# Turning the gated feed-forward rows on VectorE instead of TensorE

## What is computed

```python
def swiglu_ffn(x, norm, w_gate, w_up, w_down):
    h = rms_norm(x, norm)
    return (jax.nn.silu(h @ w_gate) * (h @ w_up)) @ w_down      # D_FF = 2816

for l in range(DEPTH_2):                                        # 2 layers
    x = x + 0.5 * swiglu_ffn(x, ffn1_norm[l], ffn1_w_gate[l], ffn1_w_up[l], ffn1_w_down[l])
    ...                                                         # mixing
    x = x + 0.5 * swiglu_ffn(x, ffn2_norm[l], ffn2_w_gate[l], ffn2_w_up[l], ffn2_w_down[l])
```

## Time and profile before

| | |
|---|---|
| median of 3 runs | 1918.7 us (1918.16 to 1920.13) |
| span of the profiled execution, first to last instruction | 1916.1 us |
| what the median has beyond that span | 2.6 us |
| TensorE busy | 1895.2 us (99%), granted clock 0.999 |
| GpSimd busy | 1361.4 us (71%) |
| ScalarE busy | 913.7 us (48%) |
| VectorE busy | 587.1 us (31%) |
| memory read | 361.5 MB, 192 GB/s over the span |

### The profile page before, as it was taken

One profiled execution on the slowest core, in us unless ns is written; L12 is line 12 of the kernel. 1 busy time (PEld: TensorE's weight loads), 2 busy tenths in 40 slices (PEclk: granted clock), 3 DMA queues, 4 the chain that ended last, 5 costly groups with the idle time before them and its releaser, 6 DMA issues.

```text
span 1916.1 us, 25277 instructions
## 1 busy us (share of the span) xinstructions
PE 1895.2 (99%) x9754; PEld 1538.9 (80%) x9754; DVE 587.1 (31%) x1061; ACT 913.7 (48%) x1365; POOL 1361.4 (71%) x568
## 2 busy tenths in 40 slices
PE   6999999999999999999999999999999999999999
PEld 3779777887787888888788888888888878888887
DVE  4213511674533410225630410110022563041011
ACT  3324511765355654355554454455445555545442
POOL 2514343456777698879678988779887967898875
PEclk9999999999999999999999999999999999999999
DMA  9662566438748476556456566557754655656653
GB/s 358 235 228 67 180 239 210 125 104 295 246 162 308 143 231 207 177 165 189 149 156 187 164 209 195 177 177 211 212 182 158 195 156 149 186 164 210 195 178 120
DMA packets 194837, 363.96 MB, mean 190 GB/s; under 512 B 32260, under 2 KB 48372, under 8 KB 194164
## 3 DMA queue, kind: packets, MB, share of 16 engines
q1 hardware_dynamic: 191280, 351.72, 57.5%
q10 hardware_dynamic: 3460, 10.88, 1.7%
HBM read 361.50 MB, written 6.10 MB: 192 GB/s over the span
## 4 chain that ended last, share of the span: by engine, by line
PE 97%; ACT 1%; DVE 1%; DMA 1%; ACTq 0%; issue 0%; POOL 0%; SPq 0%
PE ps L1140 28%; PE ps L1142 27%; PE ps L1141 27%; PE ps L1364 3%; PE ps L1158 2%; PE ps L1838 1%; PE ps L1836 1%; PE ps L1837 1%; PE ps L1185 1%; PE ps L1752 1%; PE ps L1516 1%; PE ps L1487 1%; PE ps L1497 1%; PE ps L1797 1%; PE ps L1166 1%; PE ps L1402 0%
## 5 line engine op out<-in xcount | busy, mean ns | idle before, releaser
L514 POOL TENSOR_TENSOR w_lo<-raw,w_hi 128x1024 fp32r<-128x1024 f32 x556 | 1342.4, 2447 | 508.7 <-ACT w_hi L552 485.6
L1140 PE MATMUL ps<-w_hi,xt_hi 128*128 128x512 f32 (+1 forms) x1952 | 760.2, 389 | 4.6 <-POOL w_lo L514 3.2
L1142 PE MATMUL ps<-w_hi,xt_lo 128*128 128x512 f32 (+1 forms) x1952 | 745.0, 382 | 0.0
L1141 PE MATMUL ps<-w_lo,xt_hi 128*128 128x512 f32 (+1 forms) x1952 | 744.4, 381 | 0.0
L552 ACT ACTIVATE w_hi<-raw 128x1024 fp32r<-128x1024 f32 x556 | 568.5, 1057 | 339.7 <-DMA raw<-in_ffn_w_up 101.2
L1140 PEld LDWEIGHTS ps<-w_hi,xt_hi 128*128 128x128 f32 x1952 | 367.5, 188 | 95.4 <-issue 25.6
L1142 PEld LDWEIGHTS ps<-w_hi,xt_lo 128*128 128x128 f32 x1952 | 367.3, 188 | 72.1
L1141 PEld LDWEIGHTS ps<-w_lo,xt_hi 128*128 128x128 f32 x1952 | 367.8, 188 | 65.6
L1140 PE MATMUL ps<-w_hi,xt_hi_ctx 128*128 128x512 f32 (+1 forms) x432 | 170.5, 395 | 0.2
L1142 PE MATMUL ps<-w_hi,xt_lo_ctx 128*128 128x512 f32 (+1 forms) x432 | 167.0, 386 | 0.0
L1141 PE MATMUL ps<-w_lo,xt_hi_ctx 128*128 128x512 f32 (+1 forms) x432 | 166.6, 386 | 0.0
(11 more groups left out here) (224 smaller groups left out, 1485.3 us busy)
## 6 DMA issues: line engine op xcount, KB each, us to landing
raw<-in_w_in SPq DMA_DIRECT2D x120, 512.0 KB, 3.7
raw<-in_ffn_w_gate SPq DMA_DIRECT2D x88, 512.0 KB, 4.3
raw<-in_ffn_w_up SPq DMA_DIRECT2D x88, 512.0 KB, 4.3
raw<-in_ffn_w_down SPq DMA_DIRECT2D x88, 512.0 KB, 3.2
pt<-in_ada_w SPq DMA_DIRECT2D x44, 512.0 KB, 4.8
raw<-in_pool_w_in SPq DMA_DIRECT2D x32, 512.0 KB, 8.2
raw<-in_na_w_in SPq DMA_DIRECT2D x32, 512.0 KB, 4.5
raw<-in_conv_w_in SPq DMA_DIRECT2D x32, 512.0 KB, 5.4
```

Source lines behind the costliest of these rows:

```text
L514: pool.tensor_tensor(w_lo[:, s, :], raw[:, s, :], w_hi[:, s, :].bitcast(F32), ALU.subtract).then_inc(lo_done, 1)
L1140: pe.matmul(o, h, hi, start=start, stop=False)
L1141: pe.matmul(o, h, lo, start=False, stop=False)
L1142: return pe.matmul(o, c, hi, start=False, stop=stop)
```

## The change

TensorE no longer turns the gated rows: `turn_h` and its 11 calls a pass are gone. VectorE gets a function `turned(k)` for k = 0 to 5. It turns the rows of two steps (j = 2k and 2k + 1; k = 5 has step 10 alone) by 16 `transpose` instructions, each of which takes a quarter i of the rows in `proj` and turns 32 x 32 squares into quarter q of two PSUM banks, 256 elements a partition (128 for k = 5). The banks are those that TensorE's transposes wrote. `turned(0)` and `turned(1)` stand behind the products of pairs 0 and 1; `turned(2)` behind `xt_lo` of step 1 and before the product of the rest, which itself moves from before step 4 to before step 2; `turned(3)`, `turned(4)` and `turned(5)` before steps 4, 6 and 8. DVE's loop over the pairs is written out. ACT's `high_of_hidden(j)` waits for DVE's count instead of TensorE's.

```diff
@@ high_of_hidden (ACT)
-                    act.wait_ge(pe_done, pe_s.count(("tp", key, 0, j)))
+                    act.wait_ge(dve_done, dve_s.count(("tp", key, j // 2)))
@@ ffn (TensorE)
-                def turn_h(j):
-
-                    hidden_ready(pe, name, l, j)
-                    turn(key, 0, j, lambda t, c: pj((2 * j + c) * P, P, FF, t=t), (dve_s, ("xt", key, 0, j)))
-
...
                         last.then_inc(group_used, 1)
-                        turn_h(2 * m + q)
...
-                    if j + 4 < 11:
-                        turn_h(j + 4)
@@ ffn (VectorE)
-                with dve.Fori(0, FF_PAIRS) as i:
-                    dve.wait_ge(group_used, on(g + 7 + 1, 8, i))
-                    dve.wait_ge(acc_free[(b) % 2], reads(b, i))
-                    h = pj(0, FF, FF)[:, :, bass.ds(i * 512, 512)]
-                    gated(h, 2 * ((b + 1) % 2), slice(0, 512)).then_inc(acc_free[(b + 1) % 2], 1)
                 key = f"{name}h{l}"
+
+                def turned(k):
+
+                    n = 2 if k == FF_PAIRS else 4
+                    hidden_ready(dve, name, l, 2 * k)
+                    if k >= 2:
+                        for j in range(2 * k, 2 * k + n // 2):
+                            dve.wait_ge(dve_done, dve_s.count(("xt", key, 0, j - 4)))
+                    for i in range(4):
+                        for q in range(4):
+                            rows = free(proj[32 * i:32 * i + 32, 0:1], [[P, n], [FF, NT], [1, 32]], 4 * k * P + 32 * q)
+                            to = free(ps[32 * q:32 * q + 32, 4 + 2 * (k % 2), 0:1], [[SEQ, n], [P, NT], [1, 32]], 32 * i)
+                            last = dve.transpose(to, rows)
+                    last.then_inc(dve_done, dve_s.one(("tp", key, k)))
+
+                for i in range(FF_PAIRS):
+                    dve.wait_ge(group_used, g + 8 * i + 7 + 1)
+                    dve.wait_ge(acc_free[b % 2], reads(b + 2 * i))
+                    gated(pj(i * 512, 512, FF), 2 * ((b + 1) % 2), slice(0, 512)).then_inc(acc_free[(b + 1) % 2], 1)
+                    if i < 2:
+                        turned(i)
                 for j in range(11):
-                    if j == 4:
+                    if j == 2:
+                        turned(2)
                         dve.wait_ge(act_done, act_s.count(("rest", name, l)))
                         h = pj(FF_PAIRS * 512, FF_REST, FF)
                         gated(h, 2 * (b % 2), slice(FF_REST, 2 * FF_REST)).then_inc(acc_free[b % 2], 1)
+                    if j in (4, 6, 8):
+                        turned(j // 2 + 1)
```

## The result

The changed kernel takes 1898.56 us in the median (1897.82 to 1901.5, 4 runs) beside 1918.85 us of the kernel before, a ratio of 0.9894 with the interval 0.9881 to 0.9907: 20.3 us less, where 20.5 us were forecast. A second set of runs gave 1898.73 beside 1919.53 us (changed_again).

What follows compares the result with a forecast made beforehand. TensorE, busy 1895.2 of 1916.1 us, was taken as the bound. Removing 44 turns, 5.1 us in each of four passes, saves 20.5 us with VectorE's added work hidden: 1918.7 - 20.5 = 1898.2 us, range 1895.8 to 1903.0.

Steps and rivals of the forecast that it cites:

- The bound: Whole kernel: TensorE busy 1895.2 of 1916.1 us, so an instruction taken off it is worth its step.
- The price of a turn: Four TensorE transposes cost 0.44 us in the rest stage, 0.48 in the down stage; 44 turns sum to 20.5 us.
- The time of a transpose: One VectorE transpose of 256 elements takes 0.42 us, so 6.7 us a call and about 38 us a pass.
- Call 2: turned(2), ahead of the rest's product on VectorE: ends 10.0 us after the rest starts; up to 9.9 us nothing waits.
- R: Start of the rest stage on TensorE in the first feed-forward pass, 772.25 us in the kernel before.
- the first rival: A VectorE transpose takes 0.62 to 0.85 us, turned(2) ends late, 1.0 us a pass before TensorE: 1902 us; chance 0.07.
- The chain behind it: VectorE after turned(2): low parts of steps 4, 6, 8 ready 23, 31, 37 us after the rest starts, needed at 33, 44, 55.
- the tables for the mixing add at most 1.2 us a step: VectorE in the down stage: the mixing tables lengthen its work between calls by at most 1.2 us a step.
- The waits that change: ScalarE now waits for VectorE, with weight roundings and GpSimd behind; a GpSimd lead of some 6 us stays; cost nothing.
- The point from which the change loses: At 0.85 us a VectorE transpose, the stall of a pass passes the 5.1 us gained.
- GpSimd slowed, or blocking the transposes: Two rivals: GpSimd's low parts fall back, 1910 us, chance 0.04; transposes queue behind GpSimd, 1970 us, chance 0.05.
- The advice against the change: Skill page on transpose paths: VectorE does only 32 x 32 blocks, TensorE advised for 128 x 128; no size given.

Runs made afterwards that it cites:

- all_in_two: The changed kernel with every transpose made as two of half the size, one half of all squares first; 1910.9 us, ratio 0.9951.
- call2_in_four: The changed kernel with only the third call, turned(2), made of 64 transposes of 64 elements instead of 16 of 256; 1934.35 us, ratio 1.0072.
- all_in_four: The changed kernel with every transpose made as four of 64 elements, each changing the quarter it writes; 1985.15 us, ratio 1.0343.
- calls01_in_four: The changed kernel with turned(0) and turned(1) made of 64 transposes of 64 elements, about 17.2 us each; 1898.93 us, ratio 0.9884.

## Why the prediction was right, point by point

- **The bound.** Right. TensorE stayed at 99%, and taking away, halving and doubling the turns moved the time by 20.3, 10.2 and 19.3 us.
- **The price of a turn.** 0.44 and 0.48 us, read from start times. The sum of 20.5 us stands against 20.3 (medians) and 20.4 us (from the first rest to the end). A price from the duration of the rows (4 x 0.27 us) would have given more than twice as much.
- **The time of a transpose.** 0.42 us was taken, 0.456 us measured with a step of 0.47: a call took 7.5 us instead of 6.7, the last 5.4 instead of about 4.5. The step was mis-sized by a tenth, within the bounds, and the margin took it.
- **Call 2.** Forecast to end at R + 10.0, it ended at 786.48, R + 10.4; the product of the rest was forecast from R + 12.6 to 13.5 and ran from 788.64 to 789.52, R + 12.6 to 13.5. The limit of 9.9 us for the call lies between what the runs show on both sides, 7.5 us, which cost nothing, and 10.7 us, which cost 0.2; it was 0.6 us too low. In the first pass 10.74 - 0.23 (all_in_two) and 17.23 - 6.72 (call2_in_four) both put it at 10.5 us; in the other three passes, where 17.2 us cost 6.4, it is 10.9. (In the first rival the working, 3.3 + 16 x 0.69, gives R + 14.3 and some 1.1 us a pass, not 14.2 and 1.0.)
- **The chain behind it.** Wrong in its sizes. The low parts of steps 4, 6 and 8 were forecast near R + 23, 31 and 37 and ended at R + 24, 36 and 48. Besides the longer calls the step that failed is "the tables for the mixing add at most 1.2 us a step": in the passes that make them they add up to 2.8 us before step 8, because they have two inputs in SBUF and GpSimd is nearly always busy there now (41.4 of the 43.5 us from step 0 to step 8 of the first pass; before, 39.7 of the 47.4 us, with pauses such as the idle times in the earlier trace rows). By form, the small ones (128 x 64) took 217 ns before and now

```profile
L2381 DVE TENSOR_TENSOR qt<-rope,head_gain 128x64 f32<-128x64 f32 x8 | 16.8, 2134 | 0.0
```

  2134 ns: each ends about 0.1 us after an instruction of GpSimd does. A reduction with one input in SBUF (L2369, 801.61 us) took 0.29 us beside a busy GpSimd, as before, so it was not held. The margin at step 8 shrank from 18 to 7 us, and nothing of it reached TensorE.
- **The waits that change.** "I cost all of this at nothing" held at the real call length (no new wait in a pass). But the price if the cover goes was told for VectorE's chain alone; all_in_two showed that ScalarE's queue behind the wait for a call gives way at the same length.
- **The point from which the change loses.** 0.85 us for the work of a transpose was the estimate, without the lower clock behind a wait and without the weights. The runs hold it between 0.67 us (9 us won) and 1.08 us (65 us lost).
- **GpSimd slowed, or blocking the transposes.** Neither by the transposes. GpSimd took 2.4 us a group during calls 3 and 4 of the first pass, and 3.4 us beside the two table additions of L2377 (3.1 before). The 384 transposes took 314 to 467 ns beside a busy GpSimd, and all_in_four and calls01_in_four never show one held by it. The Trainium skill, "SBUF — State Buffer", section "Who interferes with whom", said so, and the trace agrees with both halves: transposes (one SBUF input) pass, instructions with two SBUF inputs wait.
- **The advice against the change.** The prediction set the advice to use TensorE for 128 x 128 against the change (it is a rule of that page and stands outside the table that the prediction names). Here the opposite paid, because TensorE was busy for 99% of the span and VectorE for 31%.

## What to carry to other kernels

Price an instruction on the bounding engine by the step between starts, and look for an engine that idles near its place: a transpose of 0.12 us on TensorE costs VectorE two instructions of 0.47 us and was still worth moving. Then ask what stands behind each new wait in every queue, since a call that was hidden in one place cost 36 us in another, and ScalarE's queue behind a wait held up the weights of all. Moving work between engines also changes when they meet: short VectorE instructions with two inputs in SBUF waited for GpSimd's long ones.

## What the runs showed of the hardware that I had not expected

- A wait of TensorE costs more than itself: behind 6.7 us of it the next nine matmuls stepped at 0.43 instead of 0.23 us, 2.0 us more, at a granted clock of 0.50. In call2_in_four 25.8 us of waits cost 36.0, in all_in_four 62.7 cost 84.7.
- VectorE's instructions with two inputs in SBUF wait until GpSimd's running instruction has ended, whatever their own size: 0.22 us became 1.9 to 2.1 us beside `w_lo` of 2.4. It also goes the other way: a `w_lo` that began behind L2377 took 3.4 us.
- A transpose of a quarter takes 256, 323 and 456 ns for 64, 128 and 256 elements, a fixed part of about 0.19 us and 1.04 ns an element. With a change of quarter from one to the next the step is 0.27, 0.34 and 0.47 us, all of the duration; without, a step of 64 elements takes 0.13 us.
